# Token-major input projections of a two-layer encoder trunk, made in pairs with 256 moved columns

## The reference, cut to what matters

```python
def reference(x, c, ln_in_g, ...):
    ...
    for l in range(DEPTH):
        ...
        h = x * (1.0 + sc1) + sh1
        z = h @ w_in[l]
        a_u, a_v, b_cq, b_ckv, b_kr, c_u, d_q, d_f, d_i, d_g = jnp.split(z, IN_SPLITS, axis=-1)
        y_a = spatial_gating(jax.nn.gelu(a_u), jax.nn.gelu(a_v), ...)
        y_b = mla(b_cq, b_ckv, b_kr, ...)
        y_c = s5(c_u, ...)
        y_d = hgrn2(d_q, d_f, d_i, d_g, ...)
        ym = jnp.concatenate([y_a, y_b, y_c, y_d], axis=-1)...
        x = layer_norm(DN_ALPHA * x + (1.0 + g1) * (ym @ w_out[l]), ...)
        h = x * (1.0 + sc2) + sh2
        x = layer_norm(DN_ALPHA * x + (1.0 + g2) * conv_ffn(h, ...), ...)
    return x
```

## Time and profile before

| | |
|---|---|
| median of 3 runs | 1552.88 us |
| lowest, highest | 1549.14, 1557.97 us |
| the profiled execution: its time | 1546.83 us |
| its span in the profile | 1545.0 us |
| TensorE busy | 1449.7 us (94%) |
| VectorE, ScalarE, GpSimd busy | 763.3, 516.0, 496.7 us |
| mean granted TensorE clock | 0.942 of full |

### The profile page before, as it was taken

How to read it: one execution, slowest core, us unless ns; L and a number is a source line. 1 busy time by engine, 2 the same in 40 slices (tenths; PEclk the granted TensorE clock), 3 DMA queues, 4 the chain that set the end, 5 groups by cost and what they waited for, 6 DMA issues and landing times. The chain is left out here.

```text
span 1545.0 us, 17178 instructions
## 1 busy us (share of the span) xinstructions
PE 1449.7 (94%) x6860; PEld 1099.2 (71%) x6860; DVE 763.3 (49%) x1386; ACT 516.0 (33%) x784; POOL 496.7 (32%) x293
## 2 busy tenths in 40 slices
PE   6989999989999999899898999998989999989986
PEld 3446678677788888688654576867868888867865
DVE  5884753643676767632368455154353333331125
ACT  2432212342533333322242422134353333342222
POOL 0700100027644444344444010001654444443442
PEclk9999988979999999899998999697989999999998
DMA  9355522102355565454323340110213322322221
GB/s 386 118 124 163 127 96 78 46 28 82 124 177 202 178 202 179 151 190 163 112 85 87 77 73 28 28 42 4 94 54 96 96 95 96 95 82 83 95 82 55
DMA packets 69695, 168.87 MB, mean 109 GB/s; under 512 B 18672, under 2 KB 31344, under 8 KB 69104
## 3 DMA queue, kind: packets, MB, share of 16 engines
q1 hardware_dynamic: 69616, 167.78, 34.9%
HBM read 161.08 MB, written 6.67 MB: 109 GB/s over the span
## 5 line engine op out<-in xcount | busy, mean ns | idle before, releaser
L1918 POOL TENSOR_TENSOR ring_r<-ring,scr_r 128x1024 fp32r<-128x1024 f32 x148 | 355.8, 2406 | 736.9 <-ACT scr_r L1564 466.3
L437 PE MATMUL bank<-ym_r,scr_r 128*128 128x512 f32 x704 | 277.8, 395 | 5.5 <-DVE hm_r L1465 4.9
L439 PE MATMUL bank<-hm_r,scr_r 128*128 128x512 f32 x704 | 278.1, 395 | 0.0
L438 PE MATMUL bank<-ym_r,ring_r 128*128 128x512 f32 x704 | 276.9, 393 | 0.0
L437 PE MATMUL bank<-scr_r 128*128 128x512 f32 x480 | 194.1, 404 | 28.7 <-issue 14.2
L438 PE MATMUL bank<-scr_r,ring_r 128*128 128x512 f32 x480 | 192.6, 401 | 0.0
L1481 DVE SCALAR_TENSOR_TENSOR scr<-bank,pb,scr 128x511 f32<-128x511 f32 x88 | 66.0, 749 | 208.3 <-ACT scr L1796 208.2
L507 PE MATMUL bank<-hm,ring 128*128 128x512 f32 x352 | 168.0, 617 | 0.0
L437 PEld LDWEIGHTS bank<-ym_r,scr_r 128*128 128x128 f32 x704 | 132.6, 188 | 39.1 <-issue 6.5
L983 DVE SCALAR_TENSOR_TENSOR ada<-ada,silu_c 128x1024 f32<-128x1024 f32 x80 | 133.5, 1673 | 48.1 <-DMA ada<-in_w_ada 48.0
L438 PEld LDWEIGHTS bank<-ym_r,ring_r 128*128 128x128 f32 x704 | 132.4, 188 | 31.3
(11 more groups left out here) (322 smaller groups left out, 1924.9 us busy)
## 6 DMA issues: line engine op xcount, KB each, us to landing
ring<-in_w_up SPq DMA_DIRECT2D x88, 512.0 KB, 3.5
ada<-in_w_ada SPq DMA_DIRECT2D x80, 512.0 KB, 3.6
ring<-in_w_down SPq DMA_DIRECT2D x44, 512.0 KB, 3.5
ring<-in_w_in SPq DMA_DIRECT2D x34, 512.0 KB, 4.3
scr<-in_w_ada SPq DMA_DIRECT2D x16, 512.0 KB, 14.4
ring<-in_w_out SPq DMA_DIRECT2D x16, 512.0 KB, 3.5
pa<-in_par_a SPq DMA_DIRECT2D x2, 2144.5 KB, 12.8
xa<-in_x SPq DMA_DIRECT2D x1, 2048.0 KB, 8.0
```

The source lines that it names most:

```text
L437: first = mm(dst, w_hi, x_hi, start=start, stop=False)
L438: mm(dst, w_lo, x_hi, start=False, stop=False)
L439: return first, mm(dst, w_hi, x_lo, start=False, stop=stop)
L1918: G.tensor_tensor(ring_r[:, at, :], ring[:, at, :], wh[:, at, :].bitcast(F32), ALU.subtract)\
```

## The change

The two token-major projections of a pair (I0 with I1, AV0 with AV1) become one, `project_tokens`. For each token block and each slice of the contraction there is one matmul: the stationary block is loaded once, and the moved operand is 256 columns, the 128 of one ring slot and the 128 of the next. A bank then holds two token blocks of 256 features where it held four of 128. The 32 matmuls of a pair are spread over six parts as 6, 5, 5, 6, 5, 5, in the places of the three and three parts of before. Part 0 waits for both chunks. `chunk_used` is raised by one when the pair begins and by two when the projection behind the pair begins, since both slots are read to the end.

```diff
--- before.py
+++ after.py
@@ -494,21 +494,30 @@
                         chunk(l, p)
                         if p >= 4:
                             pe.wait_ge(S["proj_out"], l * NPROJ + p - 1)
-                    if WIN[p] in (I0, I1, AV0, AV1):
-
-                        for b in ((0,), (1,), (2, 3))[part]:
-                            for k in range(KD):
-                                last = mm(bank[:, b * P:(b + 1) * P], hm[:, k, b * P:(b + 1) * P], w[:, k, :],
-                                          start=(k == 0), stop=(k == KD - 1))
-                                if b == 0 and k == 0:
-                                    last.then_inc(S["chunk_used"], 1)
-                    else:
-                        for k in ((0, 1, 2), (3, 4, 5), (6, 7))[part]:
-                            last = mm(bank[:, :], w[:, k, :], hm[:, k, :], start=(k == 0), stop=(k == KD - 1))
-                            if k == 0:
-                                last.then_inc(S["chunk_used"], 2 if p == 2 else 1)
+                    for k in ((0, 1, 2), (3, 4, 5), (6, 7))[part]:
+                        last = mm(bank[:, :], w[:, k, :], hm[:, k, :], start=(k == 0), stop=(k == KD - 1))
+                        if k == 0:
+                            last.then_inc(S["chunk_used"], 2 if WIN[p - 1] in (CQ1, I1, AV1) else 1)
                     if part == 2:
                         last.then_inc(S["proj_mm"], 1)
+
+                def project_tokens(p, part):
+
+                    both = ring[:, slot(l, p):slot(l, p) + 2, :].rearrange("p j (k m) -> p j k m", m=P)
+                    if part == 0:
+                        chunk(l, p)
+                        chunk(l, p + 1)
+                        pe.wait_ge(S["proj_out"], l * NPROJ + p - 1)
+                    if part == 3:
+                        pe.wait_ge(S["proj_out"], l * NPROJ + p)
+                    for n in range((0, 6, 11, 16, 22, 27)[part], (6, 11, 16, 22, 27, 32)[part]):
+                        b, k = n // KD, n % KD
+                        last = mm(banks[(p + b // 2) % 2][:, (b % 2) * GW:(b % 2 + 1) * GW].rearrange("p (j m) -> p j m", m=P),
+                                  hm[:, k, b * P:(b + 1) * P], both[:, :, k, :], start=(k == 0), stop=(k == KD - 1))
+                        if n == 0:
+                            last.then_inc(S["chunk_used"], 1)
+                        if n % (2 * KD) == 2 * KD - 1:
+                            last.then_inc(S["proj_mm"], 1)
 
                 def level(step):
@@ -723,17 +732,17 @@
                 attend(4)
                 project(AT[Q1], 2)
                 attend(5)
-                project(AT[I0], 0)
+                project_tokens(AT[I0], 0)
                 s5_inputs()
-                project(AT[I0], 1)
+                project_tokens(AT[I0], 1)
...
@@ -1589,7 +1598,7 @@
                     j = WIN[p]
                     a.wait_ge(S["proj_mm"], l * NPROJ + p + 1)
                     bank = banks[2 + p] if p < 2 else banks[p % 2]
-                    tok = bank[:, :].rearrange("p (b n) -> p b n", n=P)
+                    tok = bank[:, :].rearrange("p (b n) -> p b n", n=GW)
                     if j in (U0, U1):
                         ins = A(ym[:, 4 + j - U0, :].rearrange("p (s x) -> p x s", s=SC),
                                 bank[:, :].rearrange("p (x s) -> p x s", s=SC), ACT.Identity)
@@ -1598,7 +1607,7 @@
                     elif j in (Q0, Q1):
                         ins = A(qt[:, j - Q0, :], bank[:, :], ACT.Identity)
                     elif j in (I0, I1):
-                        ins = A(vtok[:, :, (j - I0) * P:(j - I0 + 1) * P], tok, ACT.Identity)
+                        ins = A(vtok[:, 2 * (j - I0):2 * (j - I0) + 2, :], tok, ACT.Identity)
                     elif j in (G0, G1):
                         ins = A(ym[:, 6 + j - G0, :], bank[:, :], ACT.Identity)
                     elif j == CKV:
```

## The result

The changed kernel takes 1573.35 us, the median of 5 runs (1566.68 to 1574.11). The kernel before takes 1552.88 us in its 5 runs of the same comparison (1549.14 to 1557.97). The ratio of the run times is 1.0118 with a 95% interval of 1.0093 to 1.0144, so the change costs 18.3 us (14.4 to 22.4). That is the ratio of the means; the medians lie 20.5 us apart. The forecast was 1569 us in a range of 1557 to 1579, with a chance of 0.83 for slower: time and direction both came out as predicted.

The account below looks back on a forecast made before the run. TensorE's own work was taken to bound layer 0's mixing stage, apart from two waits. Terms -1.3 + 0.4 + 3.4 + 5.3 + 4.1 + 4.5 = +16.4 us on 1552.9 gave 1569 us, range 1557 to 1579.

Parts of the forecast that it names:

- stream: Paired projections on TensorE: 256-column matmuls save 0.4 us a pair, first half pair's gain swallowed by a wait; -1.3 us.
- uneven cut: Parts of a pair: `hg_turn` comes behind 1536 columns instead of 1024 and starts up to 1.1 us later; +0.4 us.
- wait before `level(1)`: Layer 0: modulation tile queued behind late read-backs holds up VectorE's `states(1)`, so TensorE stands 3.4 us.
- wait before `level(11)`, layer 0: Late S5 read-back starts `s5_skip` 6.3 us later; with 1.0 us slack TensorE stands 5.3 us.
- wait before `level(11)`, layer 1: Late S5 read-back starts `s5_skip` 6.2 us later; TensorE stands 4.1 us.
- clock: Behind each of three new TensorE waits, a stretch at 1.2 GHz costs 1.5 us; 4.5 us in all, bounds 0 to 9.
- The chain behind chunk 17: With T as AU0's start: load T + 1.15, writes landed T + 8.3, read-back T + 14.2, layer 0 `s5_skip` T + 14.9.
- Tile 12: Layer 0 modulation tile, queued behind eight block-matrix read-backs, lands at about 193.0 instead of 182.1 us; VectorE waits for it.
- nothing stands still: Rival at `s5_skip` and `mods_mix(12)`: DMAs land in time, only the matmul gain and the parts' cost remain; 1552 us, 8%.
- stationary blocks set the pace: Rival in the paired projections: each record costs the same whatever it moves, so half the records save 31 us; 1540 us, 3%.
- One chain only: Rival: layer 0's modulation tile slips past the read-backs and TensorE's clock stays up; +6 us, 1559 us, 9%.
- The rival of a clock that falls longer: Each new wait brings two or more half-rate stretches, spreading into VectorE chains behind; +27 us, 1580 us, 8%.

Follow-up runs that it names:

- the late release alone: Kernel before, matmuls still 128 columns wide, with only the ring slots' release moved as in the changed kernel: 1575.07 us, ratio 1.0134.
- the first experiments: Release moved in the kernel before, 1575.07 us; in the changed kernel, S5 writes moved ahead of chunk 17's load, 1562.15, block-matrix read-backs ahead of chunk 13's, 1570.05, both, 1556.71.
- The filled kernel: Changed kernel plus five matmuls of 512 columns with unused results ahead of `level(11)` in both layers: 1566.42 us, ratio 1.0091.
- the pair with the three moves: Changed kernel with block-matrix read-backs issued ahead of chunk 13's load, S5 output's writes and read-back ahead of chunk 17's: 1554.68 us, ratio 1.001.

## Why the prediction was right, term by term

| term | predicted, us | found, us |
|---|---|---|
| stream | -1.3 | -1.6: seven half pairs at 0.23, the eighth lying ahead of the first wait |
| uneven cut | +0.4 | +0.2, the wait before `hg_update` |
| wait before `level(1)` | +3.4 | +2.3 (2.4 in the second profile) |
| wait before `level(11)`, layer 0 | +5.3 | +5.1 (4.7) |
| wait before `level(11)`, layer 1 | +4.1 | +3.5 (3.6) |
| clock | +4.5 | +10.8, give or take 2.5 |
| sum | +16.4 | +20.3 by these terms; +18.3 (14.4 to 22.4) by the run times |

**The mechanism** was right in each of its steps up to the clock, and the experiments show it and not only the profile: the late release alone makes the loss, and three issues moved ahead of the two waiting loads take it away. VectorE waits for the DMAs named (and for tile 20, which the forecast left out), and TensorE for VectorE. The size of the clock's share was wrong, and that the sum came out near is in part luck.

**The chain behind chunk 17** was the best term. Load at T + 1.15, writes, read-back and `s5_skip` at T + 14.8: within 0.1 us. That worked because every link was a row of before: 7.1 us from load to last write landed and 5.9 us for the read-back. The read-back took 6.5 us in layer 0, where 5.9 and 0.7 for the two tiles had been added up. In layer 1, without tiles, the whole was 1.6 us shorter, where I had taken 1.2.

**Tile 12** landed at 192.3 us for 193.0 predicted, and the copies behind it ran on in the time forecast. The wait was 2.3 and not 3.4 us because TensorE came 0.5 us later than I had taken, behind a first wait of 3.7 instead of 3.4 us, and the tile 0.7 us sooner. The landings of before carried this well: eight read-backs took 14.1 us behind the load before, now 12.7 (178.4 to 191.1 us).

**The clock** is the term that was mis-sized. I took 1.5 us for each new wait, from the one stretch of before. To size what happened, split the mean span of the executions into span x granted clock, the time it would take at the upper level, and the rest. For before (24 executions, taken with the first experiments) that is 1456.5 + 94.2 us, for after (5) 1463.0 + 106.1: +6.5 and +11.9 us, with standard errors (what the scatter of so few executions leaves open in a mean) of 0.9 and 2.5. Of the 11.9, 1.1 is half of the 2.24 us of the longest wait that lay within a lower-clock stretch, and is counted among the waits already; that leaves 10.8 us. The stretches at the new waits explain some 5.7 of it: 1.7 us for each of the two stretches of 3.4 us, and (6.83 - 2.24) / 2 = 2.3 for the long one. The filled kernel gave 2.2 and 1.7 us back at two of these places. In the second profile of after the stretch in layer 1 lies across the wait as well, and the level behind it takes 3.06 us, so this share differs from one execution to the next. So 1.5 us apiece was only a little low, and the term was mis-sized because I looked for the clock's cost nowhere else: the other 5 us, uncertain by half their size, lie away from the new waits. In the profiled pair the 13.65 us stretch is the largest such piece, 6.2 us. Another stands behind the stage in layer 1: from 1076.0 us the clock of after is at 0.50 for 23.8 us on end, where before had it there for 3.4 and 13.6 us with 3.4 us at 1.00 between them, which makes 3.4 us more. The first piece also upsets the reading of the earlier trace rows: that the clock stays up behind the 2.0 us wait was true of the profiles of before and is not so in after, behind the same wait. The 10.8 us lie above the term's upper bound of 9, though by less than their standard error.

The clock thus took 6.3 us more than forecast. The other terms took 2.4 less: the waits 10.9 for 12.8 us, the stream and the cut half a microsecond. The terms found also add up to 2 us more than the run times show, a difference that stays open. So the errors partly cancelled. The forecast's other number shows it: for the profiled execution it gave 1563 us, and the two profiles of after took 1574.11 and 1572.94.

**The rivals.** That nothing stands still would have needed a chain under 8.5 us; it was 13.7 from the load to `s5_skip` in layer 0 and 12.1 in layer 1. That stationary blocks set the pace is refuted: half the records saved an estimated 1.8 us, not 31. The Trainium skill, "TensorE: Matmul & The Clock Gate", section "Back-to-back issue gap", lets weight loads weigh on short matmuls in a sustained stream; the float32 traces of this case do not agree, 28.26 against 28.03 us for the same columns in twice the number of blocks. One chain only did not happen: both did. The rival of a clock that falls longer comes nearest to what the clock term did, but it had the extra behind each new wait, where the profile of after shows one stretch of 3.4 us behind two of them and 6.8 across the third, and the total stayed 7 us short of its 1580.

**What stays open** is what decides whether the clock falls behind the 2.0 us wait at the end of the stage. It fell in the changed kernel and in five of the eight others made from the two, and stayed up in three, with and without new waits before it. A second profile of before and of after repeated what the first had shown, so it does not look like chance alone. Nor can its 6 us be booked in full: the pair with the three moves has the stretch, and its split is 1454.1 + 96.8 us, only 2.3 us more at the lower clock than the executions of before taken with it (94.5). The kernel with only the read-backs moved lacks the stretch, and its split is 1460.3 + 107.5 us, as much at the lower clock as the changed kernel. In the profile of after, the stretch that begins in the S5 outputs earlier in the stage lasts 23.9 us where that of before lasts 27.3, which gives 1.7 us back. How the 5 us that lie away from the new waits divide over places in the mean of the executions, one or two profiles of a kernel cannot say.

## What to carry to other kernels

When a change alters which instruction frees a buffer, do not ask first whether the load into that buffer is still in time; ask what is queued behind it. Here TensorE waited for neither of the two loads, and they cost some 18 us by holding back DMAs that had nothing to do with them. An issue that has to wait belongs behind those that are ready. And halving the number of instructions pays only where instructions, not moved columns, set the pace: read two rows of the same columns in different shapes before building it.

## What the runs showed of the hardware beyond that

The same kernel's executions spread with its clock. 24 executions of before lay between 1546.3 and 1562.9 us, at mean granted clocks from 0.945 down to 0.930, the longer mostly at the lower clock. A single profile of each kernel can thus be off by 10 us in this term; the two that I read first made a difference of 27 us out of 18.

Moved columns from two ring slots cost nothing extra: 12 such records take 2.75 us, 0.23 each, and 8 records of 256 columns from one place took 1.89 us, 0.24 each, against 1.95 / 16 = 0.12 for one of 128. The time goes by the columns in either case.

A 512 KB tile that is queued right behind the eight read-backs of small pieces takes longer to land. In the changed kernel tiles 12 and 13 took 8.3 and 8.9 us from issue to landing; in the one with the read-backs moved ahead of chunk 13's load they took 4.3 and 3.5.
